# Down projection of the MLP by seven products per part, with sums of its weights made by adding transfers

## What is computed

```python
        u = _rmsnorm(h, mlp_norm_g[l])
        h = h + jnp.square(jax.nn.relu(u @ w_up[l])) @ w_down[l]
    h = _rmsnorm(h, final_norm_g)
    return h[:, N_META:]
```

## Time and profile before

| | us |
|---|---|
| median of 3 runs | 1015.89 (1015.84 to 1016.77) |
| the profiled execution, its own time | 1016.66 |
| its span, first to last instruction | 1014.9 |

### The profile page before, as it was taken

The page is one execution under the profiler, slowest core; times in us unless marked ns, Lnnn a source line. Parts: engine busy times, 40 slices in busy tenths (PEclk is TensorE's granted clock), DMA queues, the critical chain, the costliest instruction groups (busy, mean ns, idle before and its releaser), DMA issues.

```text
span 1014.9 us, 12887 instructions
## 1 busy us (share of the span) xinstructions
PE 1004.7 (99%) x4967; PEld 849.0 (84%) x4967; DVE 522.1 (51%) x879; ACT 420.1 (41%) x689; POOL 583.9 (58%) x724
## 2 busy tenths in 40 slices
PE   9999999999999999999999999999999999999997
PEld 7888788888888888888899977888888888888886
DVE  5781256665374743445679988865123213312324
ACT  4553355555562224443246685554222222222332
POOL 4555455664756874564658878456545545545470
PEclk9999999999999999999999999999999999999999
DMA  7323222112453125323223122322322342243132
GB/s 231 115 83 100 83 84 82 44 42 84 125 169 111 56 80 189 126 83 102 64 84 109 59 84 87 95 79 94 124 87 79 104 132 76 83 130 99 63 104 83
DMA packets 84829, 99.16 MB, mean 98 GB/s; under 512 B 3698, under 2 KB 69904, under 8 KB 84768
## 3 DMA queue, kind: packets, MB, share of 16 engines
q1 hardware_dynamic: 84464, 98.07, 30.1%
q10 hardware_dynamic: 304, 0.27, 0.1%
HBM read 96.23 MB, written 2.10 MB: 97 GB/s over the span
## 4 chain that ended last, share of the span: by engine, by line
PE 92%; DVE 5%; ACT 1%; issue 1%; DVEq 0%; ACTq 0%
PE ps L455 62%; PE ps L474 19%; PE ps L865 2%; PE ps L600 1%; PE ps L524 1%; PE ps L621 1%; PE ps L585 1%; PE ps L584 1%; PE ps L662 1%; PE ps L507 0%; DVE Hl L1399 0%; DVE tmp L1896 0%; PE ps L500 0%; DVE Al L2050 0%; PE ps L691 0%
## 5 line engine op out<-in xcount | busy, mean ns | idle before, releaser
L2159 POOL TENSOR_TENSOR wlo<-raw,whi 128x256 fp32r<-128x256 f32 x648 | 505.3, 812 | 326.0 <-ACT whi L873 325.9
L873 ACT ACTIVATE whi<-raw 128x1024 fp32r<-128x1024 f32 (+1 forms) x164 | 172.2, 1050 | 148.5 <-PE ps L474 91.0
L455 PE MATMUL ps<-Hh,whi 128*128 128x512 f32 x512 | 201.9, 394 | 0.7 <-DVE Hl L1399 0.7
L455 PE MATMUL ps<-Hl,whi 128*128 128x512 f32 x512 | 199.5, 390 | 0.0
L455 PE MATMUL ps<-Ah,whi 128*128 128x512 f32 (+1 forms) x576 | 196.5, 364 | 0.2 <-DVE Al L2050 0.2
L455 PE MATMUL ps<-Al,whi 128*128 128x512 f32 (+1 forms) x576 | 194.8, 361 | 0.0
L455 PE MATMUL ps<-Hh,wlo 128*128 128x512 f32 x512 | 129.3, 389 | 0.3 <-POOL wlo L2159 0.3
L455 PE MATMUL ps<-Ah,wlo 128*128 128x512 f32 (+1 forms) x576 | 124.4, 360 | 0.0
L455 PEld LDWEIGHTS ps<-Ah,whi 128*128 128x128 f32 x576 | 103.0, 188 | 16.9 <-DVE Al L2050 0.8
L455 PEld LDWEIGHTS ps<-Al,whi 128*128 128x128 f32 x576 | 103.0, 188 | 15.9
L455 PEld LDWEIGHTS ps<-Hh,whi 128*128 128x128 f32 x512 | 96.2, 188 | 20.8 <-DVE Hl L1399 1.4
(11 more groups left out here) (309 smaller groups left out, 1187.7 us busy)
## 6 DMA issues: line engine op xcount, KB each, us to landing
raw<-in_w_in SPq DMA_DIRECT2D x29, 1024.0 KB, 5.4
raw<-in_w_up SPq DMA_DIRECT2D x16, 1024.0 KB, 5.3
raw<-in_w_down SPq DMA_DIRECT2D x32, 512.0 KB, 3.3
raw<-in_w_in SPq DMA_DIRECT2D x14, 512.0 KB, 3.7
raw<-in_w_att_out SPq DMA_DIRECT2D x4, 1024.0 KB, 5.1
raw<-in_w_sg_out SPq DMA_DIRECT2D x4, 1024.0 KB, 5.1
raw<-in_w_o SPq DMA_DIRECT2D x4, 1024.0 KB, 5.0
Fm<-in_x SPq DMA_DIRECT2D x1, 2048.0 KB, 7.8
```

Source lines behind the costliest of these rows:

```text
L455: mm = e.matmul(ps[:, bk, 0:c1 - c0], of(j)[:, k % kk, 128 * g:128 * g + 128], x[:, k, c0:c1], start=(start and n == 0), stop=(stop and n ...
L873: return e.activation(out, src, ACT.Copy, scale=scale)
L2159: ins = e.tensor_tensor(w_lo(j)[:, *cut], raw_tile(j)[:, *cut], f(w_hi(j))[:, *cut], ALU.subtract)
```

## The change

Per part, the 512 x 1024 activations and the 1024 x 1024 weights are cut into 2 x 2 quarters, and seven products of quarters (256 rows x 512 features x 512 columns) take the place of eight: `P11, P_7, P_5, P12, P_6, P_3, P_4`. A product is 24 matmuls in two weight tiles h of 256 features (`down`). Four products need a difference of activations, which DVE makes (`x_sums`), and ACT and DVE split it (`a_high`, `a_low`). Four need a sum of weight quarters: the sums are made in SBUF by transfers from `w_down` that add to what lies there, 512 KB each, begun by POOL (`w_sum`, eight per part). P_7 adds to a second copy of a quarter loaded by `load_7`; P_5, P_6 and P_4 add one quarter after another to the same place, each after the low part of the sum before has been made.

The low parts of the down weights move from POOL to DVE (`w_low`, 14 operations of 1024 elements per part). `act` becomes one DVE operation, which drains the bank, and ACT squares (`act_square`). Weights get five places instead of three. P11, P_7, P_5 and P_6 are kept in four accumulators of 1024 elements (`acc`), added up over the parts by `out`; P_3 and P_4 stay in PSUM over the four parts. In part 3 `spread_sums` first adds the accumulators of parts 0 to 2 to the quarters of the output, and `last_out` adds part 3's banks directly. The norm of the output starts after P_6, and only row blocks 2 and 3 of the left half are left for the last product. In part 0 two `residual` blocks are turned after each of the up tiles 3 to 6.

```diff
-                cols("w_down_2", 1024 * i + 256 * k, 512 * h, 1, 2, 1)
+        tiles.extend((None, (i, n, h)) for n in range(7) for h in range(2))
...
+        def w_place(part, j):
+            m = j - J_UP - 8
+            w = (whi, wlo)[part][:, (j if m < 0 else J_UP + 6 + m % 5) % 3].rearrange("p k n -> p (k n)")
+            if m >= 0 and m % 5 < 2:
+                w = w_more[:, m % 5, part]
+            return w.rearrange("p (k n) -> p k n", k=tile_rows(j))
...
+        def up_bank(part, n):
+            if part == 0 and n < 2:
+                return 4 + n
+            return 2 * ((9 * part + n // 2) % 2) + n % 2
+        def down_bank(part, n, r):
+            if n in (P_3, P_4):
+                return (4 if n == P_3 else 6) + r
+            return 2 * ((9 * part + 4 + n) % 2) + r
...
+            def load_7(part):
+                for h in range(2):
+                    r0 = 1024 * part + 256 * h
+                    src = t["w_down_2"][0][r0:r0 + 256, 512:1024]
+                    e.dma_start(w_sum3[h], src.rearrange("(k p) n -> p k n", p=128)).then_inc(
+                        *b.done("quarter7_in", (part, h), 16))
...
+                else:
+                    w.wait_ge(*low_ready(down_tile(part - 1, P11, 0)))
+                    w.wait_ge(*low_ready(down_tile(part - 1, P11, 1)))
+                    load_quarter(part, 0, 0)
+                    w.wait_ge(*low_ready(down_tile(part - 1, P_7, 0)))
+                    w.wait_ge(*low_ready(down_tile(part - 1, P_7, 1)))
+                    load_7(part)
+                    w.wait_ge(*low_ready(down_tile(part - 1, P12, 0)))
+                    w.wait_ge(*low_ready(down_tile(part - 1, P12, 1)))
+                    load_quarter(part, 1, 0)
+                    w.wait_ge(*low_ready(down_tile(part - 1, P_3, 0)))
+                    w.wait_ge(*low_ready(down_tile(part - 1, P_3, 1)))
+                    load_quarter(part, 1, 1)
+                    w.wait_ge(*low_ready(down_tile(part - 1, P_4, 1)))
+                    load_quarter(part, 0, 1)
+                load_block(up + 2)
+                load_block(up + 3)
...
+                    w.wait_ge("mlp_mean", 0)
+                    load_7(0)
...
+            def down(part, n):
+                xh, xl = x_slot(part, n)
+                kept = n in (P_3, P_4)
+                w.wait_ge("a_high", (part, n))
+                for h in range(2):
+                    j = down_tile(part, n, h)
+                    w.wait_ge("hi", j)
+                    ks = (2 * h, 2 * h + 1)
+                    for low in range(2):
+                        for r in range(2):
+                            if h == 0 and low == 0 and not (kept and part):
+                                w.wait_ge(*down_free(part, n, r))
+                            for k, x in ([(k, xh) for k in ks] if low else [(k, x) for x in (xh, xl) for k in ks]):
+                                if x is xl:
+                                    w.wait_ge("a_low", (part, n))
+                                if low:
+                                    w.wait_ge("w_low", j)
+                                of = w_lo if low else w_hi
+                                first = h == 0 and low == 0 and k == 0 and x is xh
+                                last = h == 1 and low == 1 and k == 3
+                                mm = e.matmul(ps[:, down_bank(part, n, r), :], x[:, k, 128 * r:128 * r + 128],
+                                              of(j)[:, k % 2], start=(first and not (kept and part)),
+                                              stop=(last and not (kept and part < 3)))
+                            if low and (h or r):
+                                mm.then_inc(*b.done("products", (j, r)))
+            def down_free(part, n, r):
+                if n == P_4:
+                    return "residual_set", 7 - r
+                if n == P_3:
+                    return "drained", up_tile(0, r)
+                if n in (P11, P_7):
+                    return "drained", up_tile(part, (4 if n == P11 else 6) + r)
+                return "down_out", (part, {P_5: P11, P12: P_7, P_6: P_5}[n], r)
...
+                for n in range(7 if part < 3 else 6):
+                    down(part, n)
...
+                blk, i = tiles[j]
+                if blk is not None:
+                    w.wait_ge(f"raw_in{blk % 2}", blk)
+                else:
+                    part, n, h = i
+                    if n in (P11, P12, P_3):
+                        w.wait_ge(f"quarter{int(n != P11)}{int(n == P_3)}_in", part)
+                    else:
+                        w.wait_ge(w_sum_name(n, h), (part, n))
+                m = j - J_UP - 8
+                before = j - 5 if m >= 2 else j - 3
+                if m in (0, 1):
...
+            def a_high(part, n):
+                if n in (P11, P12, P_4):
+                    w.wait_ge("act_set", (part, 3 if n == P11 else 7))
+                else:
+                    w.wait_ge("x_sum", (part, n))
+                if (part, n) > (0, 2):
+                    before = 7 * part + n - 3
+                    w.wait_ge("products", (down_tile(before // 7, before % 7, 1), 1))
+                else:
+                    w.wait_ge("products", (J_UP - 1, 3))
+                copy(x_slot(part, n)[0], x_operand(n)).then_inc(*b.done("a_high", (part, n)))
...
+            def act_square(part, n):
+                w.wait_ge("drained", up_tile(part, n))
+                e.activation(X[:, n], X[:, n], ACT.Square).then_inc(*b.done("act_set", (part, n)))
...
+            for part in range(4):
+                if part:
+                    for n in range(8):
+                        cast(up_tile(part, n) + 4)
+                        if n:
+                            act_square(part, n - 1)
+                        if n in (4, 5):
+                            a_high(part, n - 4)
+                act_square(part, 7)
+                for i in range(14):
+                    j = down_tile(part, 0, 0) + i + 4
+                    if j < n_tiles:
+                        cast(j)
+                    for n in {1: (P_5,), 2: (P12,), 4: (P_6,), 7: (P_3,), 8: (P_4,)}.get(i, ()):
+                        a_high(part, n)
...
+                if n == 0:
+                    w.wait_ge(*(("a_low", (part - 1, P_4)) if part else ("products", (J_UP - 1, 3))))
...
+                e.scalar_tensor_tensor(X[:, n], ps[:, up_bank(part, n), :], 0.0, RB, ALU.max, ALU.mult).then_inc(
+                    *b.done("drained", j))
+            def x_sums(part, n):
+                one, other, old = {P_7: (x_half(1, 0), x_half(0, 0), None), P_5: (x_half(1, 0), x_half(1, 1), None),
+                                   P_6: (x_half(0, 0), x_sum, P_5), P_3: (x_half(0, 1), x_sum, P_6)}[n]
+                w.wait_ge("act_set", (part, 3 if n == P_7 else 7))
+                if old is not None:
+                    w.wait_ge("a_low", (part, old))
+                elif part:
+                    w.wait_ge("a_low", (part - 1, P_3))
+                e.tensor_tensor(x_operand(n), one, other, ALU.subtract).then_inc(*b.done("x_sum", (part, n)))
+            def a_low(part, n):
+                w.wait_ge("a_high", (part, n))
+                low(x_slot(part, n)[1], x_operand(n), x_slot(part, n)[0]).then_inc(*b.done("a_low", (part, n)))
+            def w_low(part, i):
+                j = down_tile(part, 0, 0) + i
+                w.wait_ge("hi", j)
+                low(w_lo(j), raw_tile(j), w_hi(j)).then_inc(*b.done("w_low", j))
+            def add(y, x, op=ALU.add):
+                e.tensor_tensor(y, y, x, op).then_inc(*step())
+                w.wait_ge("vector_step")
+            def out(part, n):
+                for r in range(2):
+                    bank = ps[:, down_bank(part, n, r), :]
+                    y = y_half(0, 0)[:, r] if n == P12 else acc[acc_of[n]][:, r]
+                    w.wait_ge("products", (down_tile(part, n, 1), r))
+                    signal = b.done("down_out", (part, n, r))
+                    if n != P12 and part == 0:
+                        e.tensor_copy(y, bank).then_inc(*signal)
+                    else:
+                        w.wait_ge(*(("down_out", (part - 1, n, r)) if part else ("residual_set", 7)))
+                        e.tensor_tensor(y, bank, y, ALU.add).then_inc(*signal)
+            def last_out(n):
+                for r in range(2):
+                    bank = ps[:, down_bank(3, n, r), :]
+                    w.wait_ge("products", (down_tile(3, n, 1), r))
+                    signal = b.done("down_out", (3, n, r))
+                    if n == P_6:
+                        w.wait_ge("down_out", (3, P11, r))
+                        e.tensor_tensor(acc[3][:, r], bank, acc[0][:, r], ALU.subtract).then_inc(*signal)
+                        continue
+                    if n in (P11, P12):
+                        y, y2 = y_half(0, 0)[:, r], None
+                    else:
```

(114 more changed lines are left out.)

321 lines of the change are left out of this document (166 added, 155 removed).

## The result

The changed kernel takes 1032.86 us (median of 4 runs, 1031.03 to 1033.67) against 1016.25 us for the kernel before in the same runs: a ratio of 1.016, 95% interval 1.014 to 1.018. The forecast was 1024: the sign and the two places of the loss were right, the size was half of what came. The profiled execution took 1031.03 us, the shortest of the four, with a span of 1029.2.

What follows compares the result with a forecast made beforehand. PE, busy 99%, was taken as the bound. act(3, 6) at 960.25 - 16.3 + 9.0 = 952.9, plus DVE's 66.3 tail, gives 1019.2 against 1011.7: +7.5, called +8, so 1024 us; range 1012 to 1052 (8 in 10).

Steps and rivals of the forecast that it cites:

- the sign: Whole kernel: slower, +7.5 us worked out and called +8; chance of slower 0.66, same 0.18, faster 0.16.
- the two places of the loss: Part 0, where PE stands 9.0 us behind POOL's sums, and part 3, where DVE's tail takes 66.3 us against 51.4.
- The place and the reason of the stall: Part 0, up tile 5: POOL held until each adding transfer lands, so its low part is late; PE stands 9.0 us.
- Up tile 5 of part 1: Part 1: not late at a step of 5.3 us, late by 0.2 to 4 us from 5.8 up.
- The width of DVE's operations: DVE operations of 1024 elements on two SBUF operands: 1.23 us each, pitch 1.14, upper bound 1.41 to 1.63.
- DVE as the bound of part 3: Part 3 from act(3, 6) to the end: DVE needs 66.3 us, where PE alone would need 45.8.
- Rival 3: Whole kernel faster: step hidden behind PE, DVE's tail under 65.7 us; 1011 to 1013.6 us, chance 0.16.
- Rival 1: POOL not held, transfers hidden, no part 0 stall: -1.4 us, 1012 to 1017; without gain, 0.15 within 0.2%, 0.05 above.
- The adding transfers: POOL's eight 512 KB transfers per part: each held until the one before landed, 5.3 us a step, stalling part 0 9.0.
- The step: POOL, one issue and landing of an adding transfer: 5.3 us, 3.8 to 5.8 by the rows.
- Rival 2: Longer step makes POOL the bound: +22 at 6 us, +36 at 6.5, some +50 at 7; 1038 to 1066, chance 0.16.
- The gaps of PE in part 3: Part 3: some 8 to 9 us, first 4 to 5 at w_low behind spread_sums, next where products wait for down_out.

Runs made afterwards that it cites:

- the kernel with both edits: Changed kernel with a 2048-byte area and part 3's eight spread_sums additions placed two behind each of its first four activations: 1004.68 us, ratio to before 0.988.

## Why the prediction was half right

**Right.** The place and the reason of the stall: POOL held by each adding transfer for want of room (with 1024 bytes the next issue came 0.3 us behind each landing, the third 12.0 us behind the first; with 2048 the first three issues were over 3.8 us after the first began), the four sums of part 0 ahead of up tile 5, the first at 679.1, PE wanting the low part at 689.4 (it stood from 689.4 to 701.12). Up tile 5 of part 1 late by 0.2 to 4 us at steps from 5.8 up (1.43 at 6.0), nothing late in part 2. The width of DVE's operations, 1.23 us. DVE as the bound of part 3: the tail was put at 66.3 us and measured 67.1, and PE's last matmul came 14 us before the end. Rival 3, the gain surviving, needed a hidden step and a shorter tail, and it is what the kernel with both edits shows: at 1004.7 us it is faster than the 1011 given for it, because the additions could leave the tail altogether, which no case had considered. Rival 1, POOL not held, was priced at -1.4 us, 1015.3: the kernel with the doubled area is all but that case, and its profiled execution took 2.3 less than before (1014.39 against 1016.66).

**Wrong: the size, +7.5 worked out and +14.8 found**, both for the profiled execution. What failed is the term of one step, 5.3 us, and what hangs on it. The tail accounts for 0.8 of the difference, the way to act(3,6) for 6.5. Three terms of "The adding transfers" are in it:
- *The step.* 5.3 us was taken, the row of 1 MB; 6.0 was measured. Three steps are 2.1 us longer, the last issue 0.3 (0.76 until POOL goes on, 0.5 taken), and from there to PE's start on the low part it is 3.3 us where 2.9 were taken: 11.7 us of waiting instead of 9.0. The landing, 5.7 us, lies outside the 3.3 to 5.3 that the prediction had named as the condition of its being right. The mechanism held and the value chosen was too low: no row showed a transfer that adds, and the row taken as the upper end was none. That an adding transfer costs more than a copy, the reason for taking it, held: 1.9 times the packets, and 5.7 us to landing against 4.2. (For 5.8 the prediction gave 11 to 12, where its own terms give 10.5.)
- *The clock.* The prediction counted the wait and put what follows it at nothing. The low parts of up tiles 5 and 6 lie 8.45 us apart on PE (701.12 and 709.57) where with the doubled area they lie 6.37 apart: 2.1 us more.
- *Part 1.* The sum took nothing for it, by the step of 5.3. At 6.0 up tile 5 of part 1 waited 1.43 us, and this part ran 1.7 us longer.

Together 2.7 + 2.1 + 1.7 = 6.5. Rival 2 gave +22 for a step of 6 and was too dear by 7 us. The prediction's own terms give +10 to +14 there: 2.1 us of longer steps and 0.2 to 4 in part 1, on +7.5. In the trace POOL's eight steps and eight low parts do fit a part, and only part 1 shows a wait for them.

By the medians the loss is 16.6 us and not 14.8: the profiled execution was the shortest of its four runs. Why the changed kernel's runs spread over 2.6 us, where those of the kernel before spread over 1, is left open.

The gaps of PE in part 3 were put at 8 to 9 us and were 6.0 (4.8, 1.0 and 0.2); the first, behind the spread additions, was forecast at 4 to 5.

## What to carry to other kernels

A transfer begun by POOL held up nothing here but the next such transfer: put the work that others wait for between two of them, not behind the last, or give them room, and do not count the room by transfers: one adding transfer filled what took three copies. The same edit that frees an engine on paper has to be read as queue order: eight additions placed where DVE idled were worth 9 us, and an operation placed in idle time before its operand was there cost 2.3. When the bound moves to an engine fed by a loop of transfer, cast and operation, shorten the loop first; work taken off the engine alone came back as waiting.

## What the runs showed of the hardware

- An adding transfer of 512 KB begun by POOL: 1.21 us of issue and 5.7 us to landing; the same as a copy 0.73 and 4.2. One of 256 KB that adds took 0.88 us of issue and 4.5 to landing. With three adding ones of 512 KB under way (doubled area) the second and third took 1.70 and 2.20 us of issue and 7.6 and 9.4 to landing.
- POOL stood at the issue until an earlier transfer had landed, 4.6 to 4.8 us in the small area, and computed meanwhile if its next instruction was not a transfer (3.3 us of low parts, then 1.6 to 2.5 us of standing).
- After 11.7 us of an idle PE the granted clock was 0.50 for at least 3 us of full work, and eight matmuls took 3.78 us instead of 1.98; after the 8.7 us of the kernel with half transfers they took 3.57. After the 1.43 us in part 1 they took 2.11 with the granted clock at 1.00, so that 0.13 is not the clock's.
- DVE's operation on two operands in SBUF took 8.64 us instead of 1.22 (948.74) while POOL worked off twelve pieces of low parts without a gap (947.45 to 956.29). It cost nothing in the changed kernel, since act(3,6) came when PE's product did; in the kernel with the additions spread it took 9.86 us and held act(3,6) up by 1.2. In both it ended 1.1 us behind the last piece of POOL's row (957.38 behind 956.29, 960.00 behind 958.90), so it was out for the whole row of POOL's instructions and not for one. It is not always so: from 660.54 to 668.22 us of the same trace seven such operations of 512 elements went through beside eight pieces of POOL, 1.1 us each. What decides between the two no run here shows.
